# A block with experts: tiles of 64 rows side by side in plain fp32, and another order of the attention heads

## The reference, cut to what matters

```python
fox_out = forgetting_attention(heads(fq), heads(fk), heads(fv), log_f)   # F = cumsum(log_f)
d_out = differential_attention(q1, q2, k1, k2, v, lam)                     # p = p1 - lam * p2
d_out = rms_norm(d_out, subln) * (1.0 - lambda_init)
return jnp.concatenate([merge_heads(fox_out), merge_heads(d_out)], -1) @ w_out
```

```python
for e in range(N_EXPERTS):                       # 32
    he = jax.nn.silu(t @ w1e[e]) * (t @ w3e[e])  # 1024 -> 2 * 256
    out = out + cw[:, e:e + 1] * (he @ w2e[e])   # 256 -> 1024
```

## Time and profile before

| | |
|---|---|
| median of 3 runs | 3002.08 us (3000.64 to 3002.74) |
| profiled execution, its own time | 3001.75 us |
| its span | 2999.8 us |
| TensorE busy | 2599.3 us (87%) |
| GpSimd busy | 1164.6 us (39%) |
| mean DMA rate | 108 GB/s |
| attention, first projections to the last head's norm | about 20 to 266 us |
| router | about 2525 to 2583 us |
| experts, first memset to last down product | 2583.9 to 2941.0 us |

### The profile page before, as it was taken

One profiled execution on the slowest core, in us unless ns is written; L12 is line 12 of the kernel. 1 busy time (PEld: TensorE's weight loads), 2 busy tenths in 40 slices (PEclk: granted clock), 3 DMA queues, 4 the chain that ended last, 5 costly groups with the idle time before them and its releaser, 6 DMA issues. The chain is left out here.

```text
span 2999.8 us, 37753 instructions
## 1 busy us (share of the span) xinstructions
PE 2599.3 (87%) x14150; PEld 1964.9 (66%) x14150; DVE 1414.9 (47%) x1667; ACT 1101.4 (37%) x1450; POOL 1164.6 (39%) x524
## 2 busy tenths in 40 slices
PE   8998898799897899789879989879886897699994
PEld 5775676588774666568658877566585776566662
DVE  4335623566544432362356654334645324656663
ACT  4343422444323232242244432334322313355552
POOL 5121322343475311132234347332121432388880
PEclk9999999899998898899989999999998898799997
DMA  2111222122363110122212226221001224288872
GB/s 118 64 43 50 97 79 83 59 96 98 110 227 126 42 51 33 49 93 83 76 65 98 98 105 228 101 84 63 2 3 44 70 70 172 96 333 311 313 294 91
DMA packets 59433, 323.85 MB, mean 108 GB/s; under 512 B 12736, under 2 KB 12736, under 8 KB 36160
## 3 DMA queue, kind: packets, MB, share of 16 engines
q1 hardware_dynamic: 50112, 313.95, 28.9%
q0 software_dynamic: 9216, 8.42, 0.9%
HBM read 326.52 MB, written 20.97 MB: 116 GB/s over the span
## 5 line engine op out<-in xcount | busy, mean ns | idle before, releaser
L491 POOL TENSOR_TENSOR dense_w_lo<-weights,dense_w_hi 128x1024 fp32r<-128x1024 f32 x84 | 203.3, 2423 | 464.8 <-ACT dense_w_hi L482 464.8
L216 PE MATMUL bank<-dense_s_hi,dense_w_hi 128*128 128x512 f32 x672 | 270.3, 402 | 69.7 <-DVE dense_s_lo L452 39.8
L217 PE MATMUL bank<-dense_s_lo,dense_w_hi 128*128 128x512 f32 x672 | 267.0, 397 | 0.0
L218 PE MATMUL bank<-dense_s_hi,dense_w_lo 128*128 128x512 f32 x672 | 266.2, 396 | 0.0
L216 PE MATMUL bank<-xn_r,mix_r 128*128 128x512 f32 x480 | 194.9, 406 | 44.1 <-DVEq L1228 38.0
L482 ACT ACTIVATE dense_w_hi<-weights 128x1024 fp32r<-128x1024 f32 x84 | 88.9, 1058 | 350.5 <-PE bank L218 319.6
L216 PEld LDWEIGHTS bank<-dense_s_hi,dense_w_hi 128*128 128x128 f32 x672 | 129.5, 193 | 109.2 <-POOL dense_w_lo L491 43.8
L218 PE MATMUL bank<-xn_r,mix_r 128*128 128x512 f32 x480 | 190.3, 397 | 0.0
L1240 DVE TENSOR_TENSOR hidden<-up_y 128x512 f32 x44 | 158.9, 3611 | 63.8 <-ACT up_y L1203 63.2
L1581 DVE SCALAR_TENSOR_TENSOR xn<-mix,xn 128x1024 f32<-128x1024 f32 x64 | 121.3, 1895 | 119.7 <-DMA mix<-in_modulation 106.9
L218 PE MATMUL bank<-xn_r,weights_r 128*128 128x512 f32 x448 | 177.7, 397 | 0.0
(11 more groups left out here) (632 smaller groups left out, 6647.0 us busy)
## 6 DMA issues: line engine op xcount, KB each, us to landing
moe_weights<-in_w_experts SPq DMA_DIRECT2D x40, 1536.0 KB, 10.9
weights<-in_w_up SPq DMA_DIRECT2D x44, 1024.0 KB, 4.8
weights<-in_w_experts SPq DMA_DIRECT2D x24, 1536.0 KB, 7.1
mix<-in_modulation SPq DMA_DIRECT2D x64, 512.0 KB, 4.4
weights<-in_w_xattn SPq DMA_DIRECT2D x24, 1024.0 KB, 4.9
weights<-in_w_down SPq DMA_DIRECT2D x44, 512.0 KB, 3.6
weights<-in_w_attn SPq DMA_DIRECT2D x8, 1536.0 KB, 6.4
weights<-in_w_mlstm SPq DMA_DIRECT2D x12, 1024.0 KB, 4.9
```

Source lines behind the costliest of these rows:

```text
L216: nc.tensor.matmul(out, left.hi, right.hi, start=first, stop=False)
L217: nc.tensor.matmul(out, left.hi, right.lo, start=False, stop=False)
L218: return nc.tensor.matmul(out, left.lo, right.hi, start=False, stop=last)
L491: nc.gpsimd.tensor_tensor(w[b].lo[:, :], units.rows(b, 0, D, 0, D), w[b].hi[:, :], ALU.subtract).then_inc(w_split, 1)
```

## The change

Constants: a tile is `CAP` = 64 rows; there are always 32 main and 16 further tiles, 48 in all, worked on two at a time in 24 steps. In the list of 48 places, two main tiles are followed by one further tile. The rows of both tiles of a step are gathered and scattered by one indirect DMA each (partitions 0 to 63 and 64 to 127) and turned together; each product is done for both halves, with 64 stationary columns each, in plain fp32. The fp32r split of rows and weights goes. The loops become written-out steps, and the stage of the further tiles goes.

Weights: the up part (2 x 1 MB) and the down part (2 x 512 KB) of an expert are loaded apart, into 3 buffers for up and 4 for down. A further tile's weights come by indirect DMAs issued by GpSimd, two for up (1 MB each, one buffer) and one for down (1 MB, two buffers); for a place that no expert needs, the row numbers are out of bounds in all partitions but one.

Attention: the differential heads become units 0 to 3, the forgetting pairs 4 to 7; the gate sums are computed after the first unit's projections and needed only by unit 4.

```diff
@@ constants
-IN_FLIGHT = 4
-MORE = (2 * T - 1) // P
+ROWS_AHEAD = 4
+CAP = HALF
+MORE = 2 * T // CAP
 MOE_TILES = EXPERTS + MORE
+STEPS = MOE_TILES // 2
+MAIN_PLACE = tuple(e + e // 2 for e in range(EXPERTS))
+MORE_PLACE = tuple(3 * o + 2 for o in range(MORE))
@@ stage_attention
-FOX_UNITS = tuple(range(FOX_PAIRS))
+FOX_UNITS = tuple(range(DIFF_HEADS, DIFF_HEADS + FOX_PAIRS))
-    heads_before = lambda u: max(u - FOX_PAIRS, 0)
+    heads_before = lambda u: min(u, DIFF_HEADS)
+    place = lambda u: u - DIFF_HEADS if u in FOX_UNITS else FOX_PAIRS + u
-                if u == 0:
+                if u == FOX_UNITS[0]:
                     pe.wait_ge(forget_ready, 2)
-            project(0, 2, range(4))
+            project(0, 2)
             pe.wait_ge(log_ready, len(STARTS))
 ...
-            project(0, 2, range(4, KT))
             values(UNITS - 1)
-            head_mean(UNITS - 1)
@@ stage_router
+            for e in range(3):
+                moe.load_up(sp, e)
+                moe.load_down(sp, e)
+            moe.load_down(sp, 3)
-            for n in range(2 * TT):
-                mm = nc.tensor.matmul(g.bank[6][:, 0:MOE_TILES], by_slot[:, n, :], by_tile[:, n, :], ...)
+            for h in range(2):
+                for n in range(2 * TT):
+                    mm = nc.tensor.matmul(g.bank[6][h * HALF:(h + 1) * HALF, 0:STEPS], by_slot[:, n, :], by_tile[:, n, h:MOE_TILES:2], ...)
-            for j in range(2, TT):
+            for j in range(2, T // CAP):
 ...
+            for out, rows_each, first_row in ((moe.more_up[:, 0, :], 2 * P, 0), (moe.more_up[:, 1, :], 2 * P, P), (moe.more_down[:, :], P, 0)):
+                do(v.tensor_scalar(row[:, :], which[:, :], float(rows_each), float(first_row), ALU.mult, ALU.add))
+                do(v.tensor_scalar(row[:, :], row[:, :], g.col("partition"), g.col("last_row", rows_each // P - 1), ALU.add, ALU.min))
+                do(v.tensor_copy(out, row[:, :]))
@@ stage_experts, SyncE
+            for e in range(3, EXPERTS):
+                sp.wait_ge(up_done, main_step[e - 3] + 1)
+                moe.load_up(sp, e)
+                if e >= 4:
+                    sp.wait_ge(down_done, 2 * main_step[e - 4] + 2)
+                    moe.load_down(sp, e)
@@ stage_experts, GpSimd
+            for here in rows:
+                nc.gpsimd.memset(here, 0.0).then_inc(cleared, 1)
+            for here in (*moe.more_ups, *moe.more_downs):
+                nc.gpsimd.memset(here, 0.0).then_inc(cleared, 1)
+            pool.wait_ge(cleared, len(rows) + 4)
+            for n in range(ROWS_AHEAD):
+                gather(n)
+            load_more_up(0)
+            for o in range(2):
+                load_more_down(o)
+            for n in range(STEPS):
+                if n + ROWS_AHEAD < STEPS:
+                    pool.wait_ge(turned, 2 * n + 2)
+                    gather(n + ROWS_AHEAD)
+                for o in range(MORE - 1):
+                    if more_step[o] == n + 1:
+                        pool.wait_ge(up_done, n + 2)
+                        load_more_up(o + 1)
++                pool.wait_ge(out_read_act, n + 1)
+                pool.wait_ge(out_read_dve, n + 1)
...
+                for o in range(MORE - 2):
+                    if more_step[o] == n:
+                        pool.wait_ge(down_done, 2 * n + 2)
+                        load_more_down(o + 2)
@@ stage_experts, TensorE
+                for k in range(KT):
+                    for half, w in zip(halves, weights):
+                        mm = nc.tensor.matmul(g.bank[2 + n % 2][half, :], xt[n % 2][:, k, half],
+                                              w[k // 4][:, k % 4 * 2 * FE:(k % 4 + 1) * 2 * FE], start=(k == 0), stop=(k == KT - 1))
...
+            turn(0)
+            up(0)
+            turn(1)
+            for n in range(STEPS):
+                turn_back(n)
+                if n + 1 < STEPS:
+                    up(n + 1)
+                if n + 2 < STEPS:
+                    turn(n + 2)
+                down(n)
@@ stage_experts, ScalarE
+            read_turned(0)
+            read_turned(1)
+            read_up(0)
@@ build
-            moe = Experts(nc, inner, g.ring)
-            experts = Units(moe.ring, A["w_experts"])
-            stage_router(g, moe, experts)
-            stage_experts(g, moe, experts)
-            stage_more_experts(g, moe, experts)
+            moe = Experts(nc, inner, g, A)
+            stage_router(g, moe)
+            stage_experts(g, moe)
             stage_combine(g, moe)
```

More of the change, by code:

```diff
@@ L714, in _ @@
                     project(u + 1, 0)
-                if u > FOX_PAIRS:
+                if u > 0 and u - 1 not in FOX_UNITS:
                     head_mean(u - 1)
@@ L2424, in _ @@
         def _(sp):
-            for s in range(units.per):
-                units.load(sp, 0, s)
+            for e in range(3):
+                moe.load_up(sp, e)
+                moe.load_down(sp, e)
+            moe.load_down(sp, 3)
             for t in range(TT):
@@ L2762, in stage_experts @@
-def stage_experts(g, moe, units):
+def stage_experts(g, moe):
     nc = g.nc
-    units.begin()
-    ROUNDS = EXPERTS // IN_FLIGHT
-    HALF_UP = KT // 2 * 2 * FE
-    weights = [[moe.ring.slots[2 * u], moe.ring.slots[2 * u + 1]] for u in range(IN_FLIGHT)]
+    halves = (slice(0, HALF), slice(HALF, P))
+    main_at, more_at = ({place: i for i, place in enumerate(places)} for places in (MAIN_PLACE, MORE_PLACE))
+    main_step, more_step = [p // 2 for p in MAIN_PLACE], [p // 2 for p in MORE_PLACE]
@@ L2770, in stage_experts @@
     with ExitStack() as ctx:
-        w = Tile(g, ctx, moe, "experts", split=True)
-        block = ctx.enter_context(nc.Block())
-        def rounds(eng, step):
-            for u in range(IN_FLIGHT):
-                step(0, u, IN_FLIGHT)
-            with eng.Fori(1, ROUNDS - 1) as i:
-                for u in range(IN_FLIGHT):
-                    step(i, u, IN_FLIGHT)
-            for u in range(IN_FLIGHT):
-                step(ROUNDS - 1, u, IN_FLIGHT - 1 - u)
+        sem, sb = g.stage(ctx, "experts")
@@ L2785, in _ @@
+        silu, act_in, back = sb("silu", [P, FE]), sb("act", [P, FE]), sb("back", [P, 2, P])
+        block = ctx.enter_context(nc.Block())
         @block.sync
         def _(sp):
-            with sp.Fori(1, ROUNDS) as i:
-                for u in range(IN_FLIGHT):
-                    sp.wait_ge(w.down_done, 2 * IN_FLIGHT * i - 2 * IN_FLIGHT + 2 * u + 2)
-                    units.load(sp, i, 2 * u)
-                    units.load(sp, i, 2 * u + 1)
+            for e in range(3, EXPERTS):
[4 more added lines that the diff above has]
+                    moe.load_down(sp, e)
@@ L2793, in _ @@
         @block.gpsimd
         def _(pool):
-            w.clear(pool)
-            for u in range(IN_FLIGHT):
-                w.gather(pool, u, slice(u, u + 1), u)
-            def rest(i, u):
-                n, slot = IN_FLIGHT * i + u, 2 * (u % IN_FLIGHT) + 1
-                pool.wait_ge(w.w_rounded, 2 * n + 2)
-                pool.sem_inc(w.passed, 1)
-                nc.gpsimd.tensor_tensor(moe.ring.slots_r[slot][:, 0:HALF_UP], moe.ring.slots[slot][:, 0:HALF_UP], w.half(u % 2, 1),
-                                        ALU.subtract).then_inc(w.w_split_pool, 1)
@@ new lines, in _ @@
+            read_turned(0)
+            read_turned(1)
+            product(0)
+            for n in range(STEPS):
+                dve.wait_ge(back_turned, n + 1)
+                after(dve, down_done, 2 * n)
+                nc.vector.tensor_copy(back[:, :, :].rearrange("p a n -> p (a n)"), g.bank[4][:, 0:2 * P]).then_inc(back_read, 1)
+                if n + 1 < STEPS:
+                    product(n + 1)
+                if n + 2 < STEPS:
+                    read_turned(n + 2)
+                dve.wait_ge(down_done, 2 * n + 2)
+                after(dve, scattered[n % 2], 16 * (n // 2))
+                nc.vector.tensor_copy(out[n % 2][:, T:D], g.bank[6][:, :]).then_inc(out_read_dve, 1)
@@ L3110, in lay_out @@
     table.append(("subln", as_columns(v["diff_subln"][0])))
-    unit = [side(*(w[:, first + c + P * h:first + c + P * h + P] for c in (0, 512, 1024))) for first in (0, 1544) for h in range(4)]
+    unit = [side(*(w[:, first + c + P * h:first + c + P * h + P] for c in (0, 512, 1024))) for first in (1544, 0) for h in range(4)]
     a["w_attn"] = units_of([unit[u:u + 2] for u in range(0, UNITS, 2)])
```

492 lines of the change are left out of this document (169 added, 323 removed).

## The result

| | median (us) | ratio to the kernel before, 95% interval |
|---|---|---|
| before | 3002.12 (4 runs, 3000.64 to 3002.74) | |
| changed | 2983.37 (4 runs, 2979.66 to 2988.74) | 0.994 (0.9922 to 0.9957) |
| changed, run again beside the experiments | 2986.32 (6 runs, 2980.09 to 2995.0) | 0.9939 (0.9924 to 0.9955) |

The forecast was 2961, 41 us sooner; it came out 18.7 us sooner. The time lies in the range (2938 to 2990), but the gain is less than half of the forecast's. The executions of the changed kernel lie 9 us apart, those of before 2; in the second run it is 15 against 8. On the other chips those of before lie 10 to 12 us apart, so that it scatters more is not certain.

What follows compares the result with a forecast made beforehand. TensorE, GpSimd and the DMA engines were taken as nearly full in the experts stage. 3001.75 - 35.3 (experts) - 1.0 - 3.0 (after it) + 3.6 (router) - 5.5 (attention) = 2960.5 us; range 2938 to 2990.

Steps and rivals of the forecast that it cites:

- What bounds the stage: Experts stage: TensorE, GpSimd and the DMA engines nearly full before; after the change TensorE, with no wait for SyncE's loads.
- A step's price: Experts stage: half-wide pairs run side by side, a step takes 11.5 us; 24 steps are 276 us.
- 0.2 per change: Experts stage: if each change of tiling mode cost 0.2 us, the sum would be 17 us longer.
- Weights at 410 GB/s: Experts stage: a cycle of 3 steps loads in 33.2 us, under the 3 x 11.5 us of its steps.
- The rival with 358: Experts stage: the loads are the bound at 358 GB/s, 38.1 us a cycle, giving 2978 us; chance 0.17.
- Further tiles: Experts stage: seven waits of 2 us for further weights, 4.5 at the first pair, 3 for delayed SyncE loads.
- The step that failed in kind: Experts stage: waits of 14 + 4.5 + 3 us were added, with nothing for half rate after them.
- TensorE's clock at 1.00 through the stage: Experts stage: a sign expected in the new profile, TensorE at full granted clock throughout.
- Start: Start of experts stage: 12 pieces cleared, up(0) starts at 2602.2 with 4.6 us at half rate, up(1) ends at 2622.8.
- Router: Router: longer VectorE chains and a table product of narrow pairs, 3.6 us later (1.5 to 5.5).
- After it: End of experts stage to read back: 3 us less for the stage that goes, 1.0 for the copy before the scatter.
- Attention: Attention stage: with a forgetting pair last, net 5.5 us sooner (bounds 2 and 7).

Runs made afterwards that it cites:

- three_edits: Changed kernel with further up weights released half by half, clearing moved to the router's stage, further load issued ahead of the gather; 2958.65 us, ratio 0.9851.
- three_loads: Changed kernel, but GpSimd loads weights only for the three further places this routing fills; 2961.85 us, ratio 0.9849.

## Why the prediction was wrong

- *What bounds the stage*: right. TensorE bounds it, with SyncE's loads close behind; no step of the changed kernel waited for them.
- *A step's price*: the pair side by side is right, the size too small. Up 6.88, down 3.44, turns 0.87, turn back 0.14 and 0.10 per group gave 11.5; it is 12.0. The four changes of width cost 0.53 together, where 0.2 were counted; the groups in whole columns came to 11.47, where these terms without the 0.2 are 11.33. 22 steps: 11 us. The price that the forecast gave for 0.2 per change, 17 us in all, should by its own terms have been 14: four changes of 0.2 are 0.6 more than the 0.2 counted, in 24 steps.
- *Weights at 410 GB/s*: right (406 with the queue full). The rival with 358 falls.
- *Further tiles*: the place of the waits is right but for the last: steps 2, 5, 8 to 20 waited, step 23 did not. The landing was taken from the earlier trace rows, 4.7 at the median, from a queue at 0.82; at 0.94 the gathers take 9.7 and the further loads 6.5. The waits behind the first came to 21, not 14. Step 5 waited 7.3, where the forecast had 2 for it and 3 more for all the delay by the real further loads.
- *The step that failed in kind*: waits were counted as waits only. In the traced execution six of them, from 2.05 us up, each cost the products behind them another 1.7 to 2.8 us at half rate, 11.3 us in all (11.9 in the table above); in the second trace four did, 7.4 us. The forecast itself had priced this for the start ("With 4.6 us at half rate") and not for the waits it put into the stage. The list of signs says "TensorE's clock at 1.00 through the stage"; that was the wrong sentence.
- *Start*: right to 0.1 us at the end of up(1), by luck: up(0) ended 1.2 us sooner than forecast, and up(1) took 8.8 us, 1.7 more than at full clock, which was not in the forecast. *Router*: 1.2 in place of 3.6, just under the lower bound (the forecast's own terms add to 3.8); the narrow table product is 3.21 us, where 3.63 was and up to 3.6 more was allowed.
- *After it*: wrong in sign. Passing over the stage of further tiles cost about 1.9 us (2951.2 to 2953.1), but the drain grew by 2.6.
- *Attention*: 4.0 to 6.4 against 5.5.

Steps 11, waits 5, half rate 12, the end 4 and the attention 1.5 are 34 us too little; the drift and the router gave 5.6 back. The median is 5 us better than the traced execution. Half rate is part of such differences: the second trace of the changed kernel has 5.7 us less between its first up product and its last down product than the first (326.0 for 331.7), 4 of them at half rate and 2 of waits, though its execution was only 1.5 us shorter. What stays open is why the half by half release and the early clearing did not add up until the gather was moved too. That this depends on what is ahead in GpSimd's queue is argued and not shown: the ratios of the two runs (0.9875 and 0.9851) have overlapping intervals, and no landing was compared.

The best version, `three_edits`, is 1.5% faster than the kernel before and 0.9% faster than the change; like the change, and unlike `three_loads`, it takes any routing.

## What to carry to other kernels

Where a change puts a short wait in front of TensorE's products, price it twice: the wait, and what TensorE then runs at half rate. Here a wait of 2 us cost nearly as much again in the clock. Do not take a landing time from a trace whose queue has room if the change will fill that queue; and a load that is just in time had better go ahead of everything in its own queue that has slack (here worth 7 us, which the noise does not quite part from nothing). After an edit to the order of loads, look in the trace whether the order of the loads that are waited for did change.

## What the runs showed of the hardware

- The clock fell after waits of TensorE of 2.05 us and more in the first trace, and not after 1.89 or less; in the second trace it fell after 2.71 and not after 2.64 us, so the length alone does not decide.
- GpSimd's drain at a stage's end took 82 ns for each indirect DMA that the stage had issued (57, 64, 96), although all had landed: the last scatter landed 2.6 us after its issue, about when the drain began.
- An indirect load of 128 row numbers of which one is in bounds is not free: the further up loads, 26 of 32 of this kind, landed in 2.4 to 14.9 us, 6.5 at the median (the gathers in 9.7), and TensorE waited up to 7.3 us for one.
- Half-wide pairs run side by side at the price of one whole product (7.02 us for 8 pairs, 6.94 for 8 whole ones); each change of width costs about 0.13 us.
- One core's DMA engines moved 406 GB/s for 230 us, when TensorE's products were thinned.
